# More seven-product pairs, modulation units dealt anew, unread products left out in a two-layer diffusion backbone

## The reference, cut to what matters

```
for l in range(2):
    ctx_out = l < 1
    mod   = (silu_c  @ w_mod[l] + b_mod[l]).reshape(B, 9, 1024)   # m[0..8], for latent tokens
    mod_c = (silu_cc @ w_mod[l] + b_mod[l]).reshape(1, 9, 1024)   # mc[0..8], for context tokens
    h  = h  + 0.5*m[2]  * swiglu(modulate(rms(h),  m[0],  m[1]),  ffn1)   # silu(x Wg) * (x Wu) @ Wd
    hc = hc + 0.5*mc[2] * swiglu(modulate(rms(hc), mc[0], mc[1]), ffn1)
    y, yc = hybrid_mixer(modulate(rms(h), m[3], m[4]), modulate(rms(hc), mc[3], mc[4]), ...)
    h = h + m[5]*y
    h = h + 0.5*m[8] * swiglu(modulate(rms(h), m[6], m[7]), ffn2)
    if ctx_out:                       # the context stream ends after layer 0
        hc = hc + mc[5]*yc
        hc = hc + 0.5*mc[8] * swiglu(modulate(rms(hc), mc[6], mc[7]), ffn2)
return h
```

## Time and profile before

| | before |
|---|---|
| median of 3 executions | 1628.92 us |
| the profiled execution's own time | 1629.36 us |
| its span, first to last instruction | 1627.7 us |
| granted TensorE clock, mean over the span | 0.999 |
| TensorE (PE) busy | 1612.9 us, 99% |
| VectorE (DVE) busy | 1272.3 us, 78% |
| ScalarE (ACT) busy | 690.1 us, 42% |
| GpSimd (POOL) busy | 84.7 us, 5% |

### The profile page before, as it was taken

The page is one execution under the profiler, slowest core; times in us unless marked ns, Lnnn a source line. Parts: engine busy times, 40 slices in busy tenths (PEclk is TensorE's granted clock), DMA queues, the critical chain, the costliest instruction groups (busy, mean ns, idle before and its releaser), DMA issues.

```text
span 1627.7 us, 24207 instructions
## 1 busy us (share of the span) xinstructions
PE 1612.9 (99%) x9396; PEld 1404.6 (86%) x9396; DVE 1272.3 (78%) x1973; ACT 690.1 (42%) x1056; POOL 84.7 (5%) x149
## 2 busy tenths in 40 slices
PE   8999999999999999999999899999999999999999
PEld 4888888889878898999888798999888997999888
DVE  5887777887878679888878889888888487877654
ACT  5422233324856453333343153333333275665542
POOL 0000000110000100000000100000000000100000
PEclk9999999999999999999999999999999999999999
DMA  9454455563321224444455634444455232365554
GB/s 380 148 191 172 168 174 163 195 200 100 113 67 52 79 97 155 150 147 151 155 176 187 206 105 160 150 147 149 155 179 182 95 114 83 103 201 188 183 187 149
DMA packets 69613, 250.46 MB, mean 154 GB/s; under 512 B 7552, under 2 KB 8576, under 8 KB 69376
## 3 DMA queue, kind: packets, MB, share of 16 engines
q1 hardware_dynamic: 51072, 181.84, 33.3%
q0 software_dynamic: 18432, 67.12, 12.8%
HBM read 247.88 MB, written 1.05 MB: 153 GB/s over the span
## 4 chain that ended last, share of the span: by engine, by line
PE 92%; DVE 5%; DMA 2%; issue 1%; ACT 1%; DVEq 0%; POOLq 0%; ACTq 0%
PE ps L1699 27%; PE ps L1700 26%; PE ps L1701 26%; PE ps L1742 3%; PE ps L1790 2%; PE ps L1743 2%; DMA wm<-wmod 1%; PE ps L1792 1%; PE ps L2108 1%; PE ps L1851 1%; PE ps L2076 1%; DVE shared_b L998 1%; DVE wm L998 1%; DVE wlo L980 1%; PE ps L2090 0%
## 5 line engine op out<-in xcount | busy, mean ns | idle before, releaser
L980 DVE TENSOR_TENSOR wlo<-raw,whi 128x1024 fp32r<-128x1024 f32 x320 | 387.5, 1223 | 191.7 <-ACT whi L546 188.9
L1699 PE MATMUL ps<-xh,whi 128*128 128x512 f32 (+1 forms) x1420 | 497.1, 350 | 2.7 <-DVE xl L1185 2.3
L1700 PE MATMUL ps<-xl,whi 128*128 128x512 f32 (+1 forms) x1420 | 489.1, 344 | 0.0
L1701 PE MATMUL ps<-xh,wlo 128*128 128x512 f32 (+1 forms) x1420 | 488.8, 344 | 0.0
L546 ACT ACTIVATE whi<-raw 128x1024 fp32r<-128x1024 f32 x320 | 335.6, 1056 | 354.6 <-PE ps L1701 269.1
L1699 PEld LDWEIGHTS ps<-xh,whi 128*128 128x128 f32 x1420 | 268.7, 189 | 41.2 <-DVE xl L1185 4.4
L1701 PEld LDWEIGHTS ps<-xh,wlo 128*128 128x128 f32 x1420 | 268.7, 189 | 32.6
L1700 PEld LDWEIGHTS ps<-xl,whi 128*128 128x128 f32 x1420 | 268.9, 189 | 32.3 <-issue 0.7
L1700 PE MATMUL ps<-al,whi 128*128 128x512 f32 (+2 forms) x768 | 263.8, 343 | 0.0
L1699 PE MATMUL ps<-ah,whi 128*128 128x512 f32 (+1 forms) x668 | 236.2, 354 | 4.7 <-DVE wlo L980 2.8
L1701 PE MATMUL ps<-ah,wlo 128*128 128x512 f32 (+1 forms) x668 | 235.5, 353 | 0.0
(11 more groups left out here) (217 smaller groups left out, 2295.6 us busy)
## 6 DMA issues: line engine op xcount, KB each, us to landing
raw<-wstream SPq DMA_DIRECT2D x320, 512.0 KB, 3.5
wm<-wmod POOLq DMA_DIRECT2D x128, 512.0 KB, 4.8
wm<-wmod SPq DMA_DIRECT2D x8, 1024.0 KB, 16.8
h<-x_t SPq DMA_DIRECT2D x4, 512.0 KB, 6.4
cb<-cols SPq DMA_DIRECT2D x1, 1024.0 KB, 19.7
out_t<-h SPq DMA_DIRECT2D x8, 128.0 KB, 2.6
K<-cols SPq DMA_DIRECT2D x1, 907.0 KB, 19.9
K<-cols SPq DMA_DIRECT2D x1, 265.5 KB, 2.9
```

The lines of the kernel that those rows point to most:

```text
L980: dve.tensor_tensor(wlo[:, n % RING, :, :].rearrange("p a b -> p (a b)"), raw[:, n % RING, :], whi[:, n % SPL, :, :].rearrange("p a b -> p ...
L1699: pe.matmul(out_ap, hi_w, hi_x, start=start, stop=False)
L1700: pe.matmul(out_ap, hi_w, lo_x, start=False, stop=False)
L1701: return pe.matmul(out_ap, lo_w, hi_x, start=False, stop=stop)
```

## The change

Four things are changed.

1. **Seven-product pairs.** FFN 0 has six in place of four, FFN 1 and 2 nine in place of eight, 24 in all in place of 20. In FFN 1 and 2 the first is pair 4 (before: 5), and the last is pair 20 (before: 19).
2. **Dealing.** FFN 0 keeps units 4 to 15 (48 pairs), FFN 1 has 16 to 23 (32 pairs, before 44) and FFN 2 has 24 to 35 (48 pairs, before 36). The steps are dealt anew. Step 21, the last before the down blocks, has 2, 1 and 3 pairs of rows (before: 1, 1 and 1). FFN 2's down blocks 0 to 10 have 20 (before: 11, one each), blocks 11 to 17 have 9 (before: 3). In FFN 1's down blocks no block but block 10 has two (before: blocks 12 to 15). Step 21 of FFN 1 and 2 rounds five hidden chunks (before: three).
3. **Unread products.** From unit 28 on (`X_ONLY`) `mod_pair` leaves out the context's product: one instruction in place of two for the last 32 pairs of rows. The column it would fill is set to zero once at the start.
4. **One multiply.** `seven_mul` is one instruction of 512 columns in place of two of 256; the silu's output and `ups` are laid out in the hidden values' order for it.

```
-UNIT_AT = {0: (4, 12), 1: (16, 11), 2: (27, 9)}
+UNIT_AT = {0: (4, 12), 1: (16, 8), 2: (24, 12)}
+X_ONLY = 28
-SEVENS = ((7, 11, 15, 19), (5, 7, 9, 11, 13, 15, 17, 19), (5, 7, 9, 11, 13, 15, 17, 19))
+SEVENS = ((7, 9, 11, 14, 17, 19),
+          (4, 6, 8, 10, 12, 14, 16, 18, 20),
+          (4, 6, 8, 10, 12, 14, 16, 18, 20))
-MODS_GU = (..., 19: 2, 20: 2, 21: 1}, ..., 19: 2, 20: 2, 21: 1}, ..., 19: 2, 20: 2, 21: 1})
+MODS_GU = (..., 19: 2, 20: 2, 21: 2}, ..., 19: 2, 20: 1, 21: 1}, ..., 19: 2, 20: 1, 21: 3})
...
-           {b: 1 for b in range(14)})
+           {0: 1, 1: 2, 2: 2, 3: 1, 4: 2, 5: 2, 6: 1, 7: 2, 8: 2, 9: 2, 10: 3, 12: 2, 13: 1, 14: 2, 15: 1, 16: 2, 17: 1})
-HALVES_AT = {20: (0, 1), 21: (2, 3, 4)}
+HALVES_AT = ({20: (0, 1), 21: (2, 3, 4)},
+             {21: (0, 1, 2, 3, 4)},
+             {21: (0, 1, 2, 3, 4)})
...
             def silu_seven(f, j):
...
-                act.activation(sil[:, j % 2, 0:S], first_up[:, 0:S], ACT.Silu).then_inc(silu_a, 1)
+                act.activation(halves[:, :, 0, :], gates[:, 0, :, :], ACT.Silu)
                 act.wait_ge(gate_b, k + 1)
-                act.activation(sil[:, j % 2, S:T], first_up[:, S:T], ACT.Silu).then_inc(silu_done, 1)
+                act.activation(halves[:, :, 1, :], gates[:, 1, :, :], ACT.Silu).then_inc(silu_done, 1)
...
+            dve.memset(modc[:, X_ONLY // 2:, :, 1], 0.0)
...
             def mod_pair(u, p, junk=products):
...
-                for v in range(2):
+                for v in range(2 if u < X_ONLY else 1):
...
-                                             accum_out=flat[:, at:at + 1]).then_inc(mod_acc, 1)
+                                             accum_out=flat[:, at:at + 1])\
+                        .then_inc(mod_acc, 1 if u < X_ONLY else 2)
...
             def seven_mul(f, j):
...
-                for i in range(2):
...
+                dve.wait_ge(silu_done, FC * f + j + 1)
+                dve.scalar_tensor_tensor(hid[:, j * T:(j + 1) * T], ups, -1.0, sil[:, j % 2, :], ALU.mult, ALU.mult)                    .then_inc(mul_done, 1)
```

More of the change, by code:

```diff
@@ L79 @@
 ROWS_BANKS, TURN_BANKS = (5, 7), (6, 3)
-UNIT_AT = {0: (4, 12), 1: (16, 11), 2: (27, 9)}
+UNIT_AT = {0: (4, 12), 1: (16, 8), 2: (24, 12)}
 LATE_UNIT = 15
-SEVENS = ((7, 11, 15, 19), (5, 7, 9, 11, 13, 15, 17, 19), (5, 7, 9, 11, 13, 15, 17, 19))
[L83 to L86, removed]
-           {b: 1 for b in range(14)})
-HALVES_AT = {20: (0, 1), 21: (2, 3, 4)}
+X_ONLY = 28
+SEVENS = ((7, 9, 11, 14, 17, 19),
+          (4, 6, 8, 10, 12, 14, 16, 18, 20),
+          (4, 6, 8, 10, 12, 14, 16, 18, 20))
+MODS_GU = ({2: 1, 3: 1, 4: 2, 5: 3, 6: 1, 8: 2, 9: 1, 10: 2, 11: 1, 12: 3, 13: 1, 14: 1, 15: 3, 16: 1, 18: 2, 19: 2, 20: 2, 21: 2},
+           {1: 1, 5: 1, 7: 2, 9: 2, 11: 1, 12: 1, 13: 1, 15: 2, 17: 2, 19: 2, 20: 1, 21: 1},
+           {1: 1, 5: 1, 7: 2, 9: 2, 11: 1, 12: 1, 13: 1, 15: 2, 17: 2, 19: 2, 20: 1, 21: 3})
+MODS_DN = ({0: 1, 1: 1, 2: 1, 3: 1, 4: 1, 5: 1, 6: 1, 7: 1, 8: 1, 9: 1, 10: 2, 12: 1, 14: 1, 15: 1, 16: 1, 17: 1},
+           {0: 1, 1: 1, 2: 1, 3: 1, 5: 1, 6: 1, 7: 1, 8: 1, 9: 1, 10: 2, 13: 1, 14: 1, 15: 1, 17: 1},
+           {0: 1, 1: 2, 2: 2, 3: 1, 4: 2, 5: 2, 6: 1, 7: 2, 8: 2, 9: 2, 10: 3, 12: 2, 13: 1, 14: 2, 15: 1, 16: 2, 17: 1})
+HALVES_AT = ({20: (0, 1), 21: (2, 3, 4)},
+             {21: (0, 1, 2, 3, 4)},
+             {21: (0, 1, 2, 3, 4)})
 HALVES_DN = 5
@@ L339, in program @@
         gate_a = sem("gate_a")
-        silu_a = sem("silu_a")
         two_done = sem("two_done")
@@ L591, in silu_seven @@
                 act.activation(ups[:, 0:S], ps[:, 7, 0:S], ACT.Copy).then_inc(s1_done, 1)
+                halves = sil[:, j % 2, :].rearrange("p (s h t) -> p s h t", s=2, h=2)
+                gates = first_up.rearrange("p (h s t) -> p h s t", h=2, s=2)
                 act.wait_ge(gate_a, k + 1)
-                act.activation(sil[:, j % 2, 0:S], first_up[:, 0:S], ACT.Silu).then_inc(silu_a, 1)
+                act.activation(halves[:, :, 0, :], gates[:, 0, :, :], ACT.Silu)
                 act.wait_ge(gate_b, k + 1)
-                act.activation(sil[:, j % 2, S:T], first_up[:, S:T], ACT.Silu).then_inc(silu_done, 1)
+                act.activation(halves[:, :, 1, :], gates[:, 1, :, :], ACT.Silu).then_inc(silu_done, 1)
             def ffn(l, st):
@@ L615, in ffn @@
                         x_sums_high()
-                    for c in HALVES_AT.get(j, ()):
+                    for c in HALVES_AT[f].get(j, ()):
                         hidden_high(f, c)
@@ L1107, in seven_end @@
                 dve.tensor_tensor(first_up[:, S:T], two_ups[:, S:T], ps[:, 5, S:T], ALU.add).then_inc(gate_b, 1)
-                dve.tensor_tensor(pair_of(ups), twice(two_ups[:, 0:S]), last, ALU.add).then_inc(ups_done, 1)
+                dve.tensor_tensor(ups.rearrange("p (s h t) -> p h s t", s=2, h=2),
+                                  twice(two_ups[:, 0:S]).rearrange("p h (s t) -> p h s t", s=2),
+                                  last.rearrange("p h (s t) -> p h s t", s=2), ALU.add).then_inc(ups_done, 1)
             def seven_mul(f, j):
@@ L1113, in seven_mul @@
                 dve.wait_ge(ups_done, k + 1)
-                halves = hid[:, j * T:(j + 1) * T].rearrange("p (s h t) -> p s h t", s=2, h=2)
-                for i in range(2):
[L1116 to L1124, removed]
+                dve.wait_ge(silu_done, FC * f + j + 1)
+                dve.scalar_tensor_tensor(hid[:, j * T:(j + 1) * T], ups, -1.0, sil[:, j % 2, :], ALU.mult, ALU.mult)                    .then_inc(mul_done, 1)
             def gate_columns(m):
```

## The result

The changed kernel takes 1640.68 us (median of 4 executions, 1639.81 to 1644.9), the one before, timed beside it, 1628.78 (1628.34 to 1629.31): ratio 1.0078, 95% interval 1.006 to 1.0096. It is slower by 11.9 us. The profiled executions, 1640.07 and 1629.36, differ by 10.7.

What follows compares the result with a forecast made beforehand. TensorE was taken as the bound, with VectorE standing in order behind loads into two buffers. Terms -3.1 - 7.2 + 1.9 + 0.6 + 5.7 + 1.7 + 6.0 = +5.6 gave 1634.5 us median; own range 1630 to 1639, full range 1623 to 1642.

Steps and rivals of the forecast that it cites:

- the rival in which the loads thicken: Overlapping loads plus a weight block take 4.9 us and more each, or `tlo` of pair 4 is late: 1642 us, 13%.
- the tail: End of FFN 2, behind its down blocks: the last updates and the statistic come late, +3.6 us.
- The seven-product pairs: All three FFNs: four more such pairs save 0.78 us each, -3.1 us, if VectorE keeps up.
- pair 4: First seven-product pair of FFN 1 and 2: slack 0.8 us, cost 0; 1 to 3 us each if ScalarE's roundings slip.
- FFN 1's tail: End of FFN 1: with 32 pairs for 44 the doubled blocks 12 to 15 go, -7.2 us.
- Step 21: Modulation ahead of the hidden values down block 0 awaits: stops of +1.9, +0.6 and +5.7 us in FFN 0, 1 and 2.
- covered: Rival: step 21's hidden chunk is ready in time and the splits' run-ahead swallows the lag: 1618.6 us, 12%.
- cheap: Rival: loads come back in 3.6 us each, so FFN 2 loses less: about 1627 us, 20%.
- The clock behind the first stop: FFN 2, after the 5.7 us stop at down block 0: TensorE at half rate, +1.7 us (0 to 3).
- FFN 2's down blocks: 29 pairs for 14 make VectorE lag behind loads: +2.4 us at block 15's split, +6.0 with the end of FFN 2.
- The turn: FFN 2's down blocks: free buffer to issue, load, product; two buffers give two pairs per 6.3 us, against 5.44 per block.
- The products left out: Last 32 pairs of rows: 32 x 1.2 us less VectorE work, worth 0 by itself where VectorE waits.

Runs made afterwards that it cites:

- experiment 1: The kernel before with the 24 seven-product pairs alone and five hidden chunks rounded in step 21 of FFN 1 and 2: 1633.57 us, ratio 1.0024.
- experiment 2: As experiment 1, with the pairs of rows of steps 2 and 3 in FFN 1 and 2 put into steps 8 and 10: 1628.41 us, ratio 0.9995.
- experiment 9: The changed kernel with GpSimd's loads of modulation rows halved to 256 KB, VectorE reading the loaded half twice: 1631.30 us, ratio 1.0009.
- experiment 10: The even dealing with three pairs of rows put back into step 21 of FFN 2: 1628.64 us, ratio 0.9995.
- experiment 4: The changed kernel with one pair of rows of FFN 2 moved from step 21 to step 13: 1634.95 us, ratio 1.0033.
- experiment 8: The even dealing with the context's product computed again for the last 32 pairs of rows: 1621.14 us, ratio 0.995.
- experiment 7: The changed kernel with the context's product computed again for the last 32 pairs of rows: 1658.98 us, ratio 1.018.
- experiment 3: The kernel before with the unread context products left out and the one multiply, nothing else: 1630.38 us, ratio 1.0004.
- the even dealing: The changed kernel with 48, 40 and 40 pairs of rows, none in step 21 of FFN 1 and 2, at most two per down block: 1620.07 us, ratio 0.9945.

## Why the prediction was right, and where its sizes were off

The time came out 6.2 us above the forecast of 1634.5. That is outside the forecast's own 1630 to 1639 and inside the full range only because this reaches up to the rival in which the loads thicken (1642), to which the result is nearer. So the direction and the mechanism were right, and the size was about half of what was measured. Of the 5.1 us by which the profiled executions miss the sum, 1.4 (the mixer's +2.2 and the opening's -0.8) stand in no term at all, and the tail, for which I had 1.7 us too much, hides as much that was too little elsewhere; that is luck.

*The seven-product pairs, pair 4 and FFN 1's tail* came out to 0.1 us. That pair 4 would not stop was right with a slack that is due to the dealing, as experiments 1 and 2 show; the prediction counted without modulation there, but didn't say that the slack hung on that.

*Step 21* was right in mechanism and size: stops of 1.92, 0.60 and 5.90 for 1.9, 0.6 and 5.7. The load waited for took 4.4 us, as had been taken. The rivals in which it is covered or cheap fall with that. The Trainium skill's estimate of 3.2 us for such a load (DMA: Bandwidth & Descriptors, "Anatomy of one DMA — SWDGE (gpsimd) path") is not borne out: none of GpSimd's 126 loads of 512 KB in its loop took less than 3.6, and those of 256 KB in experiment 9 took 2.7 at least.

*The clock behind the first stop* was mis-sized: 1.7 had been read from the one window before; it was 2.4 here and 2.8 in experiment 10. And it was counted once. The stop at block 15 brought it a second time (+1.6).

*FFN 2's down blocks* carry most of the rest. Behind the first stop I had +2.4 for them, and they cost 0.67 + 1.10 + 2.81 and the 1.6 of clock, 6.2. Two steps failed. The turn of 6.3 us per two pairs holds where a load takes 4.3 (6.30 from 1236.91), but the 18 loads issued from 1194.94 to 1254.77 took 4.7 us in the mean and in the median, from 3.7 to 7.3: from the end of the first product in these blocks to the end of the twentieth it took 65.7 us (they start at 1193.01 and 1258.75) where I had 63.1, and the first was 0.9 later for the slower clock. With 4.7 in place of 4.4 a turn is 4.7 + 0.7 + 1.2 = 6.6 us, and my own sum gives 19 x 3.3 + 3 = 65.7. A number like it stood in the trace before: 4.8 in the median of all its loads. I had let a stretch of ten loads with a median of 3.8 draw it down to 4.4. The prediction had said that this term is steep, 1 us per 0.1 us of load. One issue was late as well: on the chain 1.88 us pass from 1231.02 to GpSimd's issue, where elsewhere it is 0.49; the trace does not say for what. And the first thing to be late was not the split of block 15 but `hidden_low`, which stands only two blocks ahead of its use and which I had not looked at: the two waits for `al`. Those 1.8 us may be no pure addition, since VectorE can catch up in them; no run shows how much it did.

*The tail* was +1.9 for +3.6: some of VectorE's lag had been paid at block 15.

*The mixer of layer 1* (+2.2) was not foreseen. Three weight loads issued at 1329.55, 1329.93 and 1332.79 took 6.29, 7.16 and 5.53 us, where before they took 3.75, 4.66 and 4.10, and ScalarE waited 3.7 us for the first:

```profile
1335.86 1.06 ACT L551 ACTIVATE whi<-raw 128x1024 fp32r<-128x1024 f32 x1 [3.73 <-DMA raw<-wstream]
```

The same three stand at 6.31, 7.18, 5.54 in experiment 4 and at 6.31, 7.17, 5.55 in experiment 8. In these three traces the mixer takes 185.5 to 185.8 us; in the ten others, the kernel before among them, no three such loads stand there and it takes 183.15 to 184.4. It goes with neither the dealing nor the long stops: experiment 8 has no long stop, and experiment 7, which has the most, has 183.6. What makes the loads slow stays open.

*The products left out* were worth nothing where time hides them (experiments 3 and 8), as predicted, but the sentence hides how much hung on them: with both products the same dealing costs 18 us more (experiment 7).

## What to carry to other kernels

A busy share of 78% says nothing of an engine that stands in order behind loads: with two buffers the turn is free to issue, load, product, and as many units as buffers go through per turn. Compare that turn, by the loads of the whole trace and not by those of a favourable stretch, with the time that the bound engine spends per step, and deal no step more than that; then look for the consumer with the least run-ahead, not the one that was late before. Work of this kind goes behind whatever the bound engine waits for next, not ahead of it: three pairs of rows moved into the last step cost 8.6 us.

## What the runs showed of the hardware

- The cost of half rate behind a stop does not grow in step with the stop's length. In matmuls above their usual distance, each to about 0.2 us: none behind stops of 1.80 to 2.17 us; 1.1 to 1.7 behind seven of 2.25 to 3.05; 2.3 to 2.8 behind six of 3.96 to 5.90, but 1.7 behind one of 5.36 and 2.0 behind one of 7.37 (both in experiment 7). Behind 5.90 and 7.37 the granted clock had fallen 2.0 and 2.8 us before TensorE went on, and what passes of the slow stretch while it stands costs nothing.
- The executions of a kernel with stops spread more, but not by the stops' length: those of experiments 1 and 4 lie within 7 and 8 us, those of experiment 7, with the longest stops, within 3.5, those of the even dealing within 2.6.
- Loads of 512 KB by GpSimd take over 7 us now and then (7.3, 7.5, 7.3 in the changed kernel and in experiments 4 and 10; 6.8 at most in the even dealing), and the time shows it only where VectorE has nothing in hand.
- Half the bytes take three quarters of the time (3.6 for 4.7 us in the median, experiment 9).
